# One decoder step on one core: the first modulation piece loads ahead of x, and ScalarE takes over the scaling of the heads

## The reference, cut to what matters

```python
mod = silu(c) @ w_ada + b_ada                  # six rows per sequence: sh1, sc1, g1, sh2, sc2, g2
h = rms_norm(x, norm_pre_mix) * (1 + sc1) + sh1
proj = h @ w_in                                # 1024 -> 3600 columns
ro = silu(rg) * head_layer_norm(retention(rq, rk, rv))   # 4 heads x 128
go = silu(gg) * head_rms_norm(gla(gq, gk, gv, gates))    # 4 heads x 128
x = x + g1 * rms_norm(concat(ro, go) @ w_out, norm_post_mix)
h = rms_norm(x, norm_pre_ffn) * (1 + sc2) + sh2
x = x + g2 * rms_norm(routed_experts(h) + shared_expert(h), norm_post_ffn)
```

## Time and profile before

| | |
|---|---|
| median of 3 runs | 1224.35 us |
| the profiled execution | 1225.67 us, span 1223.5 us |
| TensorE busy | 1106.1 us (90%) |
| VectorE busy | 903.4 us (74%) |
| ScalarE busy | 642.7 us (53%) |
| mean granted TensorE clock | 0.95 |

### The profile page before, as it was taken

The page is one execution under the profiler, slowest core; times in us unless marked ns, Lnnn a source line. Parts: engine busy times, 40 slices in busy tenths (PEclk is TensorE's granted clock), DMA queues, the critical chain, the costliest instruction groups (busy, mean ns, idle before and its releaser), DMA issues.

```text
span 1223.5 us, 18540 instructions
## 1 busy us (share of the span) xinstructions
PE 1106.1 (90%) x6014; PEld 811.6 (66%) x6014; DVE 903.4 (74%) x1333; ACT 642.7 (53%) x770; POOL 181.9 (15%) x185
## 2 busy tenths in 40 slices
PE   5999999999989999799999999999999999999700
PEld 3899999865444454467777777777777777777500
DVE  4422443365956777579899999989989888888878
ACT  4332221332421233257787777777777777777501
POOL 1000000000110110112222222222222222221102
PEclk9999999998879999899999999999999999999855
DMA  9542221436974143689999999999999999998996
GB/s 341 188 133 80 80 80 40 157 98 202 315 276 132 44 138 120 235 325 381 380 388 391 391 384 385 387 387 381 373 381 383 373 381 379 375 375 314 352 360 210
DMA packets 86545, 339.34 MB, mean 277 GB/s; under 512 B 12561, under 2 KB 36129, under 8 KB 59122
## 3 DMA queue, kind: packets, MB, share of 16 engines
q1 hardware_dynamic: 70130, 301.16, 67.2%
q0 software_dynamic: 16384, 37.78, 8.8%
HBM read 317.00 MB, written 42.86 MB: 294 GB/s over the span
## 4 chain that ended last, share of the span: by engine, by line
PE 46%; DMA 32%; DVE 14%; ACT 6%; issue 2%; SPq 1%; DVEq 0%; POOL 0%; POOLq 0%; ACTq 0%
DMA arena<-in_w_exp_down 28%; PE ps L1828 11%; DVE down_lo L1648 4%; PE ps L2259 4%; PE ps L2067 4%; ACT down_hi L1120 4%; PE ps L2238 3%; PE ps L2239 3%; PE ps L2240 3%; PE ps L1821 2%; PE ps L2242 1%; PE ps L2105 1%; PE ps L2226 1%; DMA arena<-expert_rows 1%; PE ps L2140 1%
## 5 line engine op out<-in xcount | busy, mean ns | idle before, releaser
L1653 DVE TENSOR_TENSOR gu_lo<-w_gu,gu_hi 128x2048 fp32r<-128x2048 f32 (+1 forms) x128 | 258.7, 2022 | 6.4 <-ACT gu_hi L1114 1.1
L1114 ACT ACTIVATE gu_hi<-w_gu 128x2048 fp32r<-128x2048 f32 (+1 forms) x128 | 217.9, 1703 | 0.0
L1648 DVE TENSOR_TENSOR down_lo<-arena,down_hi 128x2048 fp32r<-128x2048 f32 x64 | 146.7, 2293 | 58.0 <-ACT down_hi L1120 58.0
L2238 PE MATMUL ps<-gu_hi,xT_hi 128*112 128x512 f32 x448 | 182.8, 408 | 3.3 <-DVE xT_lo L1658 2.2
L2239 PE MATMUL ps<-gu_lo,xT_hi 128*112 128x512 f32 x448 | 177.9, 397 | 0.0
L2240 PE MATMUL ps<-gu_hi,xT_lo 128*112 128x512 f32 x448 | 177.3, 396 | 0.0
L1120 ACT ACTIVATE down_hi<-arena 128x2048 fp32r<-128x2048 f32 x64 | 122.7, 1918 | 64.0 <-DMA arena<-in_w_exp_down 56.1
L814 POOL DMA_INDIRECT expert_rows<-arena,row_idx x64 | 69.1, 1079 | 356.2 <-ACT arena L1159 340.1
L2259 PE MATMUL ps<-down_hi,actT_hi 128*112 128x512 f32 x256 | 106.6, 416 | 5.5 <-DVE actT_lo L1643 5.5
L807 POOL DMA_INDIRECT arena<-h_rows,token_idx x64 | 80.6, 1259 | 203.1 <-PE ps L2226 156.1
L1828 PE MATMUL ps<-w_hi,hT_hi 128*128 128x300 f32 x352 | 105.6, 300 | 1.4 <-DVE w_lo L1231 1.4
(11 more groups left out here) (310 smaller groups left out, 1989.8 us busy)
## 6 DMA issues: line engine op xcount, KB each, us to landing
w_gu<-in_w_exp_gate SPq DMA_DIRECT2D x64, 1024.0 KB
w_gu<-in_w_exp_up SPq DMA_DIRECT2D x64, 1024.0 KB
arena<-in_w_exp_down SPq DMA_DIRECT2D x64, 1024.0 KB
arena<-in_w_ada SPq DMA_DIRECT2D x16, 1024.0 KB, 6.9
arena<-in_w_in SPq DMA_DIRECT2D x12, 1200.0 KB, 5.6
arena<-expert_rows SPq DMA_DIRECT2D x9, 1024.0 KB, 13.4
arena<-in_w_ada_first SPq DMA_DIRECT2D x4, 2048.0 KB, 16.2
arena<-expert_rows SPq DMA_DIRECT2D x4, 2048.0 KB, 13.0
```

What stands on the lines that cost most here:

```text
L1114: a.activation(gu_hi[b % RING][:, :, ks], w_gu[b % U][:, :, ks], ACT.Copy).then_inc(s_ghi, 1)
L1648: v.tensor_tensor(down_lo[:, :, :], w_dn[b % RING], down_hi[:, :, :].bitcast(F32), ALU.subtract).then_inc(s_dlo, 1)
L1653: v.tensor_tensor(gu_lo[b % U][:, :, ks], w_gu[b % U][:, :, ks], gu_hi[b % RING][:, :, ks].bitcast(F32), ALU.subtract).then_inc(s_glo, 1)
L2238: pe.matmul(out, x_hi, gu_hi[r][:, :, k], start=(k == 0), stop=False)
```

## The change

On SP, modulation piece 0 is loaded ahead of all tiles of x, and w_in group 2 ahead of the large block of constants. On TensorE, product and columns of piece 0 come ahead of the transposes; in the rest of the front the product of piece c+1 comes between the two k of the projection of piece c, not behind both; and products whose result nothing reads (`idle_products`, of width 320 into bank 6, and of width 512 into bank 5) are put at places where the engine waits. On ScalarE, `mod1_rows(0)` comes ahead of the squares, and the split of w_in group 0 ahead of the modulated transpose. On VectorE, `low_part(0, 0)` moves between the two steps of the modulated low part. In GLA, ScalarE multiplies the eight heads of each prompt tile by their reciprocal roots (`heads_scaled`), which takes two of the seven instructions of `heads` from VectorE; `heads(t)` now waits for that (`s_ng`).

```diff
+            load_mod1(0)
             for t in range(2):
                 sp.dma_start(x_tile[t], tok_rows(x_prompt, x_sample, t)).then_inc(s_x[t], 16)
...
-            load_mod1(0)
             win = w_in[0].rearrange("(k p) n -> p k n", p=P)
...
+            sp.wait_ge(s_wlo, 2)
+            load_win(2)
             sp.dma_start(arena[:, FIRST_W:CONST_W], consts[:, FIRST_W:CONST_W]).then_inc(s_const, 16)
...
+            mod1_rows(0)
             square(0)
             square(1)
+            xT_first_half(0)
             square(2)
-            xT_first_half(0)
             square(3)
...
             for c in range(NC1):
-                mod1_rows(c)
-                hT_high_part(c)
                 if c == 0:
                     high_part(0, 0)
+                else:
+                    mod1_rows(c)
+                hT_high_part(c)
...
+            def heads_scaled(t):
+                a.wait_ge(s_nr, t + 1)
+                for n, at in enumerate((C_RQ, C_GO)):
+                    for h in range(H):
+                        cols = slice(at + h * DV, at + (h + 1) * DV)
+                        o = a.activation(proj[:, t, cols], proj[:, t, cols], ACT.Copy, scale=head_rs[:, t, n * H + h:n * H + h + 1])
+                o.then_inc(s_ng, 1)
...
                 if t == PT:
                     mixed_T(0)
+                    heads_scaled(t - 1)
                 a.wait_ge(s_go, t + 1 if t < PT else PT + H)
                 if t < PT:
                     gla_T(t + 1)
+                    if t:
+                        heads_scaled(t - 1)
...
-                a.activation(proj[0:R, t, C_GG:C_GG + RET_W], proj[0:R, t, C_GG:C_GG + RET_W], ACT.Silu).then_inc(s_ng, 1)
+                o = a.activation(proj[0:R, t, C_GG:C_GG + RET_W], proj[0:R, t, C_GG:C_GG + RET_W], ACT.Silu)
+                if t == PT:
+                    o.then_inc(s_ng, 1)
...
-                hT_low_part(c)
+                hT_whole_part(c)
                 if c == 0:
                     low_part(0, 0)
+                hT_low_part(c)
...
-                    step(v.tensor_tensor(o3, o3, head_rs[0:R, t, n * H:(n + 1) * H].unsqueeze(2).broadcast_to([R, H, DV]), ALU.mult))
+                    if t == PT:
+                        step(v.tensor_tensor(o3, o3, head_rs[0:R, t, n * H:(n + 1) * H].unsqueeze(2).broadcast_to([R, H, DV]), ALU.mult))
...
+            def idle_products(n, bank, width=FIRST_W):
+
+                for _ in range(n):
+                    pe.matmul(ps[:, bank, 0:width], ident, arena[:, 0:width], start=True, stop=True)
+
+            idle_products(4, 6)
...
+            mod1_product(0)
+            idle_products(1, 6)
+            mod1_columns(0)
             for t in range(NT):
+                idle_products((2, 2, 4, 1, 1)[t], 6)
                 x_tile_transposed(t)
-            mod1_product(0)
-            mod1_columns(0)
+            idle_products(6, 6)
+            pe.wait_ge(s_wlo, 1)
+            project_first(0, (0,))
             mod1_product(1)
-            pe.wait_ge(s_wlo, 1)
+            project_first(0, (1,))
             mod1_columns(1)
-            project_first(0)
             mod1_product(2)
+            project_first(1, (2,))
             mod1_columns(2)
-            project_first(1)
             mod1_product(3)
+            project_first(1, (3,))
             mod1_columns(3)
-            project_first(2)
-            project_first(3)
+            project_first(2, (4, 5))
+            project_first(3, (6, 7))
...
+                    if h == H - 1:
+                        idle_products(2, 5, 512)
                     if 2 * h + half:
                         pe.wait_ge(s_rkve, 2 * h + half)
...
+            idle_products(2, 5, 512)
             pe.wait_ge(s_rste, 1)
```

More of the change, by code:

```diff
@@ L560, in _ @@
             sp.dma_start(r_bias[:, :], router_bias[0:1, :].broadcast_to([P, E])).then_inc(s_small, 16)
-            with sp.Fori(2, NG) as g:
+            with sp.Fori(3, NG) as g:
                 sp.wait_ge(s_wlo, g)
@@ L1209, in mod1_fold, with hT_whole_part @@
                 mark(v.scalar_tensor_tensor(out=scale1[:, ks], in0=scale1[:, ks], scalar=1.0, in1=wide(2), op0=ALU.add, op1=ALU.mult), s_fold, c + 1)
-            def hT_low_part(c):
-                ks = slice(2 * c, 2 * c + 2)
+            def hT_whole_part(c):
                 if c == 0:
@@ L1218, in hT_low_part @@
                 step(o)
+            def hT_low_part(c):
+                ks = slice(2 * c, 2 * c + 2)
                 v.wait_ge(s_hT, NT + 2 * c + 2)
@@ L1244, in _ @@
             v.tensor_copy(condT_wide[:, :, 0:NCOND], ps[:, 7, 0:KT * NCOND].rearrange("p (k c) -> p k c", k=KT)).then_inc(s_cTs, 1)
-            step(v.tensor_copy(condT[:, :, :], ps[:, 7, 0:KT * NCOND].rearrange("p (k c) -> p k c", k=KT)))
+            v.tensor_copy(condT[:, :, :], ps[:, 7, 0:KT * NCOND].rearrange("p (k c) -> p k c", k=KT)).then_inc(s_cTs, 1)
             x_scaled(0)
@@ L1287, in _ @@
                     low_part(i * 2 + (b + 2), b)
+            v.wait_ge(s_const, 32)
             for g in range(6, NG):
@@ L1754, in _ @@
             o.then_inc(s_cT, 1)
-            pe.wait_ge(s_cTs, 1)
+            def idle_products(n, bank, width=FIRST_W):
+                for _ in range(n):
+                    pe.matmul(ps[:, bank, 0:width], ident, arena[:, 0:width], start=True, stop=True)
+            idle_products(4, 6)
+            pe.wait_ge(s_cTs, 2)
             def mod1_product(c):
@@ L1797, in x_tile_transposed, with project_first @@
                     o.then_inc(s_tr, 1)
-            def project_first(c):
-                for k in (2 * c, 2 * c + 1):
+            def project_first(c, ks):
+                for k in ks:
                     pe.wait_ge(s_hT, NT + 2 * c + 2)
@@ L1812, in project_first @@
                         o = pe.matmul(ps[:, PT, 0:GW], hT_sample[:, k], w[:, k], start=(k == 0 and n == 0), stop=(k == KT - 1 and n == 1))
-                if c == NC1 - 1:
+                if k == KT - 1:
                     o.then_inc(s_pj, 1)
```

1 line of the change is left out of this document (removed).

## The result

The changed kernel takes 1240.26 us (median of 4 executions, 1239.57 to 1242.55), the kernel before 1225.12 us (4 executions, 1218.88 to 1226.07). The ratio is 1.0134, with a 95% interval of 1.0105 to 1.0163: 15.1 us slower between the medians, where 10.5 were forecast.

What follows compares the result with a forecast made beforehand. The kernel was taken as bound by a chain of waits, 46% TensorE, 32% DMA, 14% VectorE. Front +5.0, retention -0.7 and GLA +6.2 summed to +10.5 us, so a median of 1234.8 us, range 1221.5 to 1241.

Steps and rivals of the forecast that it cites:

- the clock that retention would win back: End of retention: a clock kept at its higher level from about 289.4 to 299.6 us gives back 4.0 us.
- the two stalls of GLA: GLA: output of tile 2 comes 3.5 us late, and the first output half waits 2.7 us for w_out.
- Load order and x chain: Front: piece 0 loaded first shifts x by 6.1 us; the first projection product starts 3.35 us later.
- Pieces ahead of products: Front, first projection product to group 1: 26.1 us in place of 23.0, so 3.1 us worse.
- the early load of group 2: End of the front: loading w_in group 2 earlier gives back TensorE's idle time of 1.4 us.
- Unread products in retention: End of retention: three pairs add 3.3 us to the chain, the higher clock gives 4.0 back: -0.7 us.
- I take both: Retention: counting both the 3.3 us added and the 4.0 us the clock gives back, for -0.7 us.
- ScalarE scales the heads: GLA: VectorE idles before heads, then w_out is late: 3.5 + 2.7 = +6.2 us, bounds 2.5 and 7.5.
- rival 2: The clock stays high throughout, in retention and GLA; the sum falls by 7.7 to +2.8 us, 1227.2; chance 0.15.
- Rival 1: Front: x is late by under 1 us, front -2.2, total +3.3 us, 1227.6; chance 0.15.
- Rival 3: Scaling never delays VectorE, GLA -4.3 us, front at its lower bound, or rivals 1 and 2 together; near 1219; chance 0.12.
- Rival 4: Everything at its upper bound: front +8.3, retention +3.3, GLA +7.5, total +19 us, 1243; chance 0.08.

Runs made afterwards that it cites:

- f1: The kernel before with only the change's front (load order, engine orders, unread products there), retention and GLA as before: 1225.25 us.
- r1: The kernel before with only the three pairs of unread products of width 512 at the end of retention: 1227.85 us.
- g1: The kernel before with only the scaling of heads on ScalarE, placed in GLA as in the change: 1235.9 us.
- p1: The kernel before with the change's front but without any unread product, retention and GLA as before: 1228.19 us.
- h1: The kernel before with only ScalarE's scaling, late (behind the wait for tile 1's output) for tile 0, early for tiles 1 to 3: 1230.77 us.
- h2: The kernel before with only ScalarE's scaling, late (behind the mixed transposes' copies) for tile 3, early for tiles 0 to 2: 1230.48 us.
- c1: The kernel before with only ScalarE's scaling, heads_scaled(t-1) placed ahead of its wait for the output of tile t: 1226.05 us.
- e1: The kernel before with six unread products of width 512 in TensorE's GLA wait for modulation pieces 14 and 15: 1224.34 us.

## Why the prediction was right and where it was wrong

The direction, the place and the mechanism of the main loss were forecast; the size was 15.1 for 10.5. The parts as measured are -0.4, +3.9 and +10.8, together 14.3, where the forecast had +5.0, -0.7 and +6.2. The steps that failed are three terms of the sum: the late x chain of the front, the clock that retention would win back, and what follows the two stalls of GLA. The first was too high by 5.4, the other two too low by 4.6 each, so that the total came as near as it did is in part luck.

The two profiles by themselves would have hidden this: group 2 starts 4.4 us later, retention adds 3.9, and the GLA stage 6.4. That looks like the forecast's front, and only the times of f1, r1 and g1 and the further traces show otherwise.

- **Load order and x chain** (+3.35 forecast, -2.0 measured between the means of the traces). What failed is the price of the transposes: I kept 1.9 and 1.95 us for each of the first two tiles, and 4.55 for the last three. That was in part the lower clock level, and the unread products ahead of them took it away (p1): the last transposes end at 24.1 and not at 28.95, and from there the 6.3 us to the first projection product are as forecast (6.4). The pair of x was misjudged too, though it did not set tile 2's start in my sum (21.6 against 23.3): it came 3.1 us late, 3.9 between the means, and not 6.1. I had read 6.1 off the landings of two loads that overlapped, which is not the time by which one of them holds up the other. The lower bound, 4.8 by the rate of the windows, was nearer. The Trainium skill, page "DMA: Bandwidth & Descriptors", section "Where 436 GB/s comes from", puts the rate of the fabric at 435 GB/s, by which the transfer is an estimated 4.8 us as well. The windows of 426 and 451 GB/s above agree with that rate, and not with the 358 GB/s that the same section gives as the limit for loads from HBM.
- **Pieces ahead of products** (+3.1 forecast, +3.4 measured from the first product to group 1, between means; -1.6 between means for the early load of group 2, forecast -1.4). This step was right. In the one trace after, the stretch is 7.7 us longer; the clock is low there from 30 to 33 and from 44 to 50.
- **Unread products in retention** (-0.7 forecast, +3.9 measured). The 3.3 us added are there, as 3.7 in the traces. The step "I take both" failed: the 4.0 given back exist only in an execution whose clock would fall at 290, and the profile before happened to be one. Three of eleven traces were so in full. The upper end of my bounds, +3.3, is what most executions pay.
- **ScalarE scales the heads.** Every local number held: VectorE idle 5.08 (5.0 forecast), eight scalings 2.44 (2.4), output of tile 2 later by 3.6 (3.5), the wait for w_out 2.84 (2.7). What was mis-sized, +10.8 measured (6.2 to 15.3) for +6.2, is what follows each, put at nothing: h1 gives +5.1 for the stall put at 3.5, h2 +6.1 for the end put at 2.7. In the trace after, TensorE is at its lower level from 324 to 344 behind the first stall (before from 320 to 327). At the end the second output half starts 12.5 us after the first, where it was 7.7: 4.8 more, of which 2.84 are the wait, and 2.0 the lower level behind it (2.89 for 1.72 in the last two products, 1.65 for 0.87 in eight transposes). I had worked out prices of the lower level for rival 2, but only as something to be won. The shorter last load, 10.92 for 13.16, gave 2 us back.
- **Rival 1** (x not late) came near for the front (-2.2; the measured -0.4 has an interval from -2.7 to +2.0), but not by its mechanism: x was late, by 3.1 us and not by under 1. **Rival 2** (the clock stays high) is refuted in GLA (0.50 from 324 to 344). **Rival 3** supposed that an early scaling wins 1.44 per tile; c1 shows that the early place wins nothing that can be measured (+0.6, -1.7 to +2.9). Its own terms (+0.9, -0.7 and -4.3) also sum to 1220.2, not to 1219. **Rival 4** fits retention and GLA best, where its bounds of 3.3 and 7.5 were even passed by the middle values (3.9 and 10.8), and is wrong in the front (+8.3).

Not settled by time is how much of g1's 10.8 is the clock and how much the stall. The half width of an interval here is 2 to 5 us, as wide as that effect.

## What to carry to other kernels

When work moves to an engine that has time to spare, its place in that engine's order decides: the same eight instructions cost 10.8 us behind a wait for the next tile's output and nothing that could be measured ahead of it. A stall of TensorE is priced with what runs behind it at the lower clock level: at the end of GLA 2.84 us of wait made 4.8. The times of h1 and h2, 5.1 and 6.1 for stalls put at 3.5 and 2.7, point the same way, with intervals too wide for a factor. Before a saving is read from one trace's low clock, look at a second trace of the same kernel.

## What the runs showed of the hardware that I had not expected

- In the middle of a kernel, the same TensorE program is at 1.2 GHz for some 10 us at the start of GLA in some executions and at 2.4 in others, with 4.2 us between them; group 2 of the projection starts anywhere from 70.7 to 76.2 us in nine traces of one front.
- At the start of the span the windows show a clock of 1.00 (p1, 6 to 14 us), while the product of piece 0 takes 3.64 us there and 1.92 in the change: there the durations tell the level and the column does not. From 17 us on it shows 0.50, and the transposes are slow as well (3.58 for 16).
- Products that nothing reads are no cure in themselves: filled waits moved the fall of the clock behind the next wait (e1), and three pairs in waits of 0, 0.8 and 1.2 us cost 3.9 (r1).
